# One level of Strassen's product for the FFN up projection, with the norm factor put into the activations

## The chip, the cores and the metric

The kernel runs on one core of a Trainium2 chip. The metric is device time in microseconds (us) of one execution; lower is better. Engines are named as in the profile: PE (TensorE, matmuls; PEld its weight loads), DVE (VectorE), ACT (ScalarE), POOL (GpSimd), SP (SyncE, which issues the DMAs here).

## The reference

The kernel computes a two-layer trunk over 1024 positions of width 1024 in float32. Each layer has an attention mixer and a gated FFN with a causal depthwise convolution; both layers have the same FFN, with their own weights:

```python
D_MODEL = 1024; SEQ = 1024; D_FF = 2816; CONV_WIDTH = 3

def conv_ffn(h, w_up, conv_w, conv_b, w_down):
    u = h @ w_up
    y = conv_b
    for j in range(CONV_WIDTH):
        y = y + conv_w[j] * _shift(u, CONV_WIDTH - 1 - j)
    a, g = jnp.split(y, 2, axis=-1)
    return (jax.nn.silu(g) * a) @ w_down

def reference(x, ...):
    h = x
    for i in range(DEPTH):
        n = rmsnorm(h, attn_norm_g[i])
        m = dsa_mixer(...) if i % N_MIXERS == 0 else chunk_band_mixer(...)
        h = h + m @ w_out[i]
        h = h + conv_ffn(rmsnorm(h, ffn_norm_g[i]), w_up[i], conv_w[i], conv_b[i], w_down[i])
    return h
```

## The kernel before

The program is a row of phases: `head_phase`, `select_phase`, `dsa_phase`, `ffn_phase` for layer 0, `band_phase`, `ffn_phase` for layer 1. The change concerns the two FFN phases. The residual stays in SBUF as XT, transposed: 8 blocks (db) of 128 model columns by 1024 positions.

**Arithmetic.** PE multiplies in fp32r. Each float32 operand is split into a high part (a copy by ACT to fp32r) and a low part (operand less high, by POOL or DVE), and each product is three matmuls: high x high, high weight x low activation, low weight x high activation. One matmul is 128x128 weights by 128x512 activations.

**Up projection.** The 5632 columns of w_up are 44 chunks of 128, ordered so that chunks 2m and 2m + 1 are the value and the gate of the same 128 hidden columns; two of them are called a pair here, and there are 22 pairs. `up` (L359) takes one chunk: for 8 db, 3 products and 2 halves of the positions, 48 matmuls at L375 into one of two PSUM pairs (UP), 128x1024. DVE multiplies the result by RB, the norm's factor of every position spread over the partitions, into U (L423). ACT starts Y as u times the last tap plus the bias (L283), DVE adds the two shifted taps (L425, L431), ACT applies silu to the gate (L287), DVE multiplies (L437), ACT and POOL split the product into AH and AL (L291, L330).

**Down projection.** Two pairs are a group. `down` (L381) multiplies the group's two hidden chunks: 8 db x 2 chunks x 3 x 2, 96 matmuls at L391, and DVE adds each 128x1024 result to XT (L413).

**Weights.** A ring of four chunks: SP loads WR (512 KB each, L241), ACT makes WH (L268), POOL WL (L322), two chunks ahead of PE. The order on each engine is the order in which the program writes it; engines meet by semaphores. A loop of five turns holds two groups each: 4 chunks, down of the group before, 4 chunks, down.

**Start of a phase.** XH and XL are XT times the norm's gain, split by ACT (L139) and DVE (L145). The norm's factor isn't in them: while PE multiplies, the sums of squares are joined (L160, L163), summed over partitions by sixteen small matmuls (L152), turned into a factor by DVE and POOL (L167, L172), put on diagonals (DG, L450), spread by PE (L354) and copied to RB (L277). It is needed only at L423.

Of the kernel before, what the change touches and what calls it, by code (L numbers as in the profile page):

```python
# [17 lines left out]
P = 128  # L18
D = 1024
# [12 lines left out]
UPC = 2 * PAIRS  # L32
CHUNKS = NGRP * (UPC + PAIRS)
RING = 4
# [58 lines left out]
class Squares:  # L93
# [5 lines left out]
    def __init__(self, c, sem, xsq=None):  # L99
        self.c = c  # L100
        self.XSQ = c.XSQ if xsq is None else xsq
        self.squared, self.even, self.odd = sem("squared_x"), sem("even_added"), sem("odd_added")
# [5 lines left out]
    def add(self, eng, db):  # L108
# [5 lines left out]
        acc = c.ACC[:, db % 2, :]  # L114
# [7 lines left out]
class Norm:  # L122


    def __init__(self, c, stage, m, sem, bank, last_square):
        self.c, self.stage, self.LAST = c, stage, last_square
        self.squared = sem("n_squared")
        self.VAR = m.take(f"VAR{stage}", [P, TT], F32)
# [19 lines left out]
    def tensor(self, pe):  # L148
        c = self.c
        pe.wait_ge(self.joined, 2)  # L150
        for t in range(TT):
            mm = pe.matmul(self.SS[:, t:t + 1], c.ACC[:, 0, t * P:(t + 1) * P], c.ONES[:, 0:1], start=True, stop=True)  # L152
        mm.then_inc(self.summed, 1)
# [4 lines left out]
    def join(self, dve):  # L158
        c = self.c
        dve.tensor_tensor(c.ACC[:, 0, :], c.ACC[:, 0, :], c.ACC[:, 1, :], ALU.add).then_inc(self.joined, 1)  # L160
        dve.wait_ge(self.joined, 1)
        dve.wait_ge(self.squared, 1)
        dve.tensor_tensor(c.ACC[:, 0, :], c.ACC[:, 0, :], self.LAST, ALU.add).then_inc(self.joined, 1)  # L163
# [11 lines left out]
def ffn_phase(nc, c, layer, stage, stream, out=None, w_next=None):  # L175
# [4 lines left out]
    with ExitStack() as ctx:  # L180
        sem, old = c.signals.open(ctx, f"f{layer}")
        m = Map(nc, c.scratch, c.end)
        WR = c.chunks[layer].W
        m.at += RING * 4 * D
        WH = m.take(f"WH{layer}", [P, RING, D], F32R)
        WL = m.take(f"WL{layer}", [P, RING, D], F32R)
        Y = m.take(f"Y{layer}", [P, PAIRS, 2, S], F32)
        AH = m.take(f"AH{layer}", [P, 2, PAIRS, S], F32R)
        AL = m.take(f"AL{layer}", [P, 2, PAIRS, S], F32R)
        U = m.take(f"U{layer}", [P, 2, S], F32)  # L190
        RB = m.take(f"RB{layer}", [P, S], F32)
        DG = m.take(f"DG{layer}", [P, TT, P], F32)
        norm = Norm(c, stage, m, sem, c.bank[7], Y[:, 0, 0, :])
        squares = Squares(c, sem) if out is None else None
        UP = [c.pair[1], c.pair[0]]
        DN = c.pair[2:4]
        landed = [sem(f"landed{i}") for i in range(RING)]
        w_hi, w_lo = sem("w_hi"), sem("w_lo")
        up_ready, biased, tap1, convolved = sem("up_ready"), sem("biased"), sem("tap1"), sem("convolved")
        scaled, diag_ready, spread, rb_ready = sem("scaled"), sem("diag_ready"), sem("spread"), sem("rb_ready")  # L200
# [3 lines left out]

        PER = UPC + PAIRS
        LOOPS = (NGRP - 1) // 2
        TURN = 2 * PER
        AHEAD = 2
        EARLY = c.chunks[layer].count
        assert CHUNKS == UPC + LOOPS * TURN + PAIRS and TURN % RING == 0  # L210

        def at(it, per_turn, n):

            return n if it is None else it * per_turn + n

        def up_at(n):

            return n + max(n // UPC - 1, 0) * PAIRS

        def down_at(g):  # L220

            return UPC + (g + 1) * PER - PAIRS if g < NGRP - 1 else CHUNKS - PAIRS

        def wait_weights_used(eng, it, ch):

            g, k = divmod(ch - UPC, PER)
            if ch < UPC:
                eng.wait_ge(up_ready, at(it, 2 * UPC, ch + 1))
                if it is not None:
                    eng.wait_ge(dn_free, at(it, 2 * DB, 2))  # L230
            elif k < UPC:
# [2168 lines left out]
```

## Time and profile before

| | before |
|---|---|
| median of 3 runs | 2798.01 us (2797.06 to 2799.74) |
| the profiled execution: time | 2800.03 us |
| the profiled execution: span | 2797.9 us |
| PE busy | 2700.6 us, 97% |
| DVE busy | 1426.0 us, 51% |
| ACT busy | 1118.5 us, 40% |
| POOL busy | 918.5 us, 33% |
| mean granted clock of PE | 0.989 of full speed |
| matmuls at L375 and L391 | 4224 and 2112 |

The span is the time from the first to the last instruction of the profiled execution. PE's busy time is of pipelined matmuls: one lasts 0.39 us, though the next starts earlier. The first FFN phase lies at about 694 to 1436 us, the second from 2055 us to the end.

### The profile page before, as it was taken

How to read it: one execution, taken by the hardware profiler on the slowest of the kernel's cores; microseconds unless marked ns; L12 is line 12 of the kernel's file. 1: busy time of each engine (PE TensorE's matmuls, PEld its weight loads, DVE VectorE, ACT ScalarE, POOL GpSimd, SP SyncE). 2: the span in 40 equal slices, each digit the busy share in tenths (PEclk: the TensorE clock that was granted, in tenths of full speed). 3: DMA queues.
4: the chain of work that ended last, by engine and by line, in shares of the span. 5: the costliest groups of instructions: out<-in, count | busy, mean ns of one | idle time of the engine just before them, and what ended most of it. 6: DMA issues, size and time to landing. Idle time of an engine off the chain costs nothing. (4 is left out here: it accounts for less than half of the span.)

```text
span 2797.9 us, 38917 instructions
## 1 busy us (share of the span) xinstructions
PE 2700.6 (97%) x14518; PEld 2347.8 (84%) x14518; DVE 1426.0 (51%) x2492; ACT 1118.5 (40%) x2415; POOL 918.5 (33%) x639
## 2 busy tenths in 40 slices
PE   7799899999999999999999999999989999999999
PEld 6599788887788888888889999999868888888887
DVE  5899777741554444444441114666145444444444
ACT  5687666642322222222245446777123222222221
POOL 2134433103332223322244444564223332322322
PEclk9899999999999999999999999999999999999999
DMA  5100000101111111111121111334111111111111
GB/s 175 46 29 22 24 9 9 65 27 49 46 53 53 45 45 45 53 52 45 46 101 46 46 46 30 87 90 133 38 53 46 46 47 58 45 52 45 45 52 60
DMA packets 71012, 147.13 MB, mean 53 GB/s; under 512 B 7824, under 2 KB 44864, under 8 KB 69216
## 3 DMA queue, kind: packets, MB, share of 16 engines
q1 hardware_dynamic: 70880, 145.38, 16.4%
q8 instruction: 82, 1.34, 0.2%
q14 instruction: 50, 0.41, 0.1%
HBM read 122.22 MB, written 13.69 MB: 49 GB/s over the span
## 5 line engine op out<-in xcount | busy, mean ns | idle before, releaser
L375 PE MATMUL banks<-XH,WH 128*128 128x512 f32 x1408 | 438.4, 393 | 21.3 <-POOL WL L322 12.6
L322 POOL TENSOR_TENSOR WL<-WR,WH 128x1024 fp32r<-128x1024 f32 x132 | 328.1, 2493 | 376.8 <-ACT WH L268 376.8
L375 PE MATMUL banks<-XH,WL 128*128 128x512 f32 x1408 | 436.9, 392 | 0.0
L375 PE MATMUL banks<-XL,WH 128*128 128x512 f32 x1408 | 436.5, 391 | 0.0
L283 ACT ACTIVATE Y<-U,CONVB,CONVW 128x1024 f32<-128x1024 f32 x88 | 109.5, 1244 | 630.4 <-DVE U L423 630.4
L375 PEld LDWEIGHTS banks<-XH,WH 128*128 128x128 f32 x1408 | 265.6, 189 | 79.3 <-POOL WL L322 13.4
L423 DVE TENSOR_TENSOR U<-banks,RB 128x1024 f32<-128x1024 f32 x88 | 107.7, 1224 | 410.6 <-PE banks L375 395.6
L375 PEld LDWEIGHTS banks<-XH,WL 128*128 128x128 f32 x1408 | 266.3, 189 | 55.7
L375 PEld LDWEIGHTS banks<-XL,WH 128*128 128x128 f32 x1408 | 266.1, 189 | 55.7
L330 POOL TENSOR_TENSOR AL<-Y,AH 128x1024 fp32r<-128x1024 f32 x44 | 105.9, 2407 | 608.6 <-ACT AH L291 608.6
L413 DVE TENSOR_TENSOR XT<-XT,banks 128x1024 f32<-128x1024 f32 x176 | 214.4, 1218 | 165.0 <-PE banks L391 165.0
L391 PE MATMUL banks<-AH,WH 128*128 128x512 f32 x704 | 219.3, 393 | 0.0
L391 PE MATMUL banks<-AL,WH 128*128 128x512 f32 x704 | 217.2, 390 | 0.0
L391 PE MATMUL banks<-AH,WL 128*128 128x512 f32 x704 | 216.9, 389 | 0.0
L268 ACT ACTIVATE WH<-WR 128x1024 fp32r<-128x1024 f32 x132 | 136.1, 1046 | 193.4 <-PE banks L391 101.9
L431 DVE SCALAR_TENSOR_TENSOR Y<-U,CONVW,Y 128x1022 f32<-128x1022 f32 x88 | 197.1, 2240 | 8.8 <-DVE Y L425 0.9
L425 DVE SCALAR_TENSOR_TENSOR Y<-U,CONVW,Y 128x1023 f32<-128x1023 f32 x88 | 113.0, 1284 | 137.2 <-ACT Y L283 137.2
L391 PEld LDWEIGHTS banks<-AH,WH 128*128 128x128 f32 x704 | 130.6, 188 | 31.5 <-DVE XT L413 5.5
L391 PEld LDWEIGHTS banks<-AL,WH 128*128 128x128 f32 x704 | 132.2, 188 | 27.9
L391 PEld LDWEIGHTS banks<-AH,WL 128*128 128x128 f32 x704 | 132.2, 188 | 27.8
L2092 PE MATMUL banks<-QW,XH 128*128 128x384 f32 x512 | 132.0, 338 | 16.4 <-POOL QW L2040 16.4
L1015 DVE TENSOR_SCALAR QVAR<-SSQ 128x4 f32<-128x4 f32 x64 | 20.5, 320 | 208.7 <-ACT JUNK L712 208.7
(264 smaller groups left out, 5528.5 us busy)
## 6 DMA issues: line engine op xcount, KB each, us to landing
WR<-in_ffn SPq DMA_DIRECT2D x132, 512.0 KB, 3.5
HT<-HC SPq DMA_DIRECT2D x224, 64.0 KB, 2.0
QWR<-in_qkv SPq DMA_DIRECT2D x8, 1536.0 KB, 6.5
XT<-in_xT SPq DMA_DIRECT2D x16, 512.0 KB, 7.8
OWR<-in_w_o SPq DMA_DIRECT2D x16, 512.0 KB, 3.3
QWR1F<-in_qkv SPq DMA_DIRECT2D x4, 1536.0 KB, 6.2
spill<-XT SPq DMA_DIRECT2D x8, 512.0 KB, 11.3
XT<-spill SPq DMA_DIRECT2D x8, 512.0 KB, 7.1
```

The costliest lines, as they stand in the source:

```text
L268: act.activation(WH[:, ch % RING, :], WR[:, ch % RING, :], ACT.Copy).then_inc(w_hi, 1)
L283: act.activation(Y[:, j, k, :], U[:, k, :], ACT.Identity, bias=c.CONVB[:, layer, bass.ds(tap, 1)], scale=c.CONVW[:, layer, 2, bass.ds(tap, ...
L322: pool.tensor_tensor(WL[:, ch % RING, :], WR[:, ch % RING, :], WH[:, ch % RING, :].bitcast(F32), ALU.subtract).then_inc(w_lo, 1)
L330: pool.tensor_tensor(AL[:, g % 2, j, :], Y[:, j, 0, :], AH[:, g % 2, j, :].bitcast(F32), ALU.subtract).then_inc(a_lo, 1)
L375: mm = pe.matmul(u[:, h * HALF:(h + 1) * HALF], w[:, ch % RING, db * P:(db + 1) * P], x[:, db, h * HALF:(h + 1) * HALF], start=(db == 0 an ...
L391: mm = pe.matmul(DN[db % 2][:, h * HALF:(h + 1) * HALF], w[:, (ch + j) % RING, db * P:(db + 1) * P], x[:, g % 2, j, h * HALF:(h + 1) * HAL ...
L413: dve.tensor_tensor(c.XT[:, db, :], c.XT[:, db, :], DN[db % 2][:], ALU.add).then_inc(dn_free, 1)
L423: dve.tensor_tensor(U[:, k, :], UP[k][:], RB[:], ALU.mult).then_inc(scaled, 1)
L425: dve.scalar_tensor_tensor(Y[:, j, k, 1:S], U[:, k, 0:S - 1], c.CONVW[:, layer, 1, bass.ds(tap, 1)], Y[:, j, k, 1:S], ALU.mult, ALU.add).t ...
L431: dve.scalar_tensor_tensor(Y[:, j, k, 2:S], U[:, k, 0:S - 2], c.CONVW[:, layer, 0, bass.ds(tap, 1)], Y[:, j, k, 2:S], ALU.mult, ALU.add).t ...
L1015: dve.tensor_scalar(VAR[:, t % 2, :], SSQ[:, t % 2, :], 1.0 / HD, EPS, ALU.mult, ALU.add).then_inc(var_ready, 1)
L2092: mm = pe.matmul(PJ[t % len(PJ)][:, 0:PROJ], x[:, db, i * P:(i + 1) * P], w[:, k % 2, db, :], start=(db == 0 and x is c.XH and w is WH), s ...
```

## The change

The FFN phase is written anew around `Pair`, the two chunks of one pair.

- **Seven products.** A pair's weights are 1024 model rows by 256 columns. They are cut into quarters A11, A12 (first chunk, model rows 0 to 511 and 512 to 1023) and A21, A22 (second chunk). The activations are cut into quarters too: model rows by positions 0 to 511 and 512 to 1023. One quarter product is 4 blocks x 3 = 12 matmuls into one PSUM bank. Eight would be needed; `seven` does seven, with four sums of weight quarters (POOL, L579, once per pair: 128x512 each) and four sums of activation quarters T1 to T4 (once per layer). The sums of the results are made partly by PE, which accumulates two products in one bank, and partly by DVE (`u2`, `c22`, `c21`, `c12`: 5 additions of a bank and a 128x512 piece of U) and ACT (two copies, `first_copy`, `second_copy`). Pair 0 is done with eight products (`classic`), 96 matmuls, pairs 1 to 21 with 84.
- **Norm factor.** The factor RB is now multiplied into the activations, with the gain, before they are split (`scale_x`, L771, DVE). So no activation exists before the factor does; the multiplication of the results (L423 before) is gone.
- **Weights.** Highs and lows are made for each of the seven quarters (or sums), 128x512, in a ring of six slots (WH, WL). The raw chunks are loaded into one place (RAW, two chunks), as soon as the last low of the pair before is made. Down projection weights come as four halves of 256 KB, which take four slots.
- **Order.** The loop has nine turns: seven products of a first pair, a down projection, seven products of a second pair. The next turn's first pair follows directly. After the loop come two pairs and two down projections.
- The squares' accumulators of the FFN's norm lie elsewhere (FFN_ACC); the input arrays `up` and `down` are apart. The loads of the first two chunks in the phase ahead are as before.

The core of the diff:

```diff
+UP = 7
+CLASSIC = 4
+DOWN = 4
+TURN = 2 * UP + DOWN
+SLOTS = 6
+LOOPS = NGRP - 2
+LAST = 2 * NGRP - 1
...
-        WH = m.take(f"WH{layer}", [P, RING, D], F32R)
-        WL = m.take(f"WL{layer}", [P, RING, D], F32R)
+        WH = m.take(f"WH{layer}", [P, SLOTS, HALF], F32R)
+        WF = nc.alloc_sbuf_tensor_at(f"WF{layer}", [P, SLOTS, HALF], F32, offset=m.at)
+        WL = m.take(f"WL{layer}", [P, SLOTS, HALF], F32R)
...
+        A11, A12, A21, A22 = raw(0, 0), raw(0, 1), raw(1, 0), raw(1, 1)
+        S3_AT, S4_AT = A21, A11
+        def source(pair, k):
+            return (A11, full(pair.slot + 1), full(pair.slot + 2), S3_AT, A12, A22, S4_AT)[k]
...
+            def load_pair(it, p):
+                pair, before = Pair(it, p), Pair(it, p - 1)
+                sp.wait_ge(w_lo, CLASSIC if p == 1 else before.slots(UP))
+                for k in range(2):
+                    sp.dma_start(RAW[:, k, :], up[pair.tap(k)]).then_inc(raw_landed, 16)
...
+            def upper(it, p):
+                pair, nxt, ahead = Pair(it, p - 1), Pair(it, p), Pair(it, p + 1)
+                weights_high(nxt, 4, 5)
+                bias(pair)
+                first_copy(nxt)
+                weights_high(nxt, 6)
+                silu(pair)
+                split(pair)
+                weights_high(ahead, 0)
+                second_copy(nxt)
+                weights_high(ahead, 1, 2, 3, 4)
...
+            def first_sums(pair):
+                pool.wait_ge(raw_landed, pair.at(32, 32 * pair.p))
+                wait_slot(pool, pair.it, pair.slot + 1)
+                sum_of(pair, full(pair.slot + 1), A21, A22, ALU.add)
+                pool.wait_ge(w_sum, pair.sums(1))
+                sum_of(pair, S3_AT, A11, A21, ALU.subtract)
+            def second_sums(pair):
+                wait_slot(pool, pair.it, pair.slot + 2)
+                pool.wait_ge(w_sum, pair.sums(2))
+                sum_of(pair, full(pair.slot + 2), A22, S3_AT, ALU.subtract)
+                pool.wait_ge(w_sum, pair.sums(3))
+                pool.wait_ge(w_lo, pair.slots(1))
+                sum_of(pair, S4_AT, A12, full(pair.slot + 2), ALU.subtract)
...
+            def product(pair, k, bank, i, first):
+                n = (pair.slot + k) % SLOTS
+                pe.wait_ge(w_lo, pair.slots(k + 1))
+                for b in range(4):
+                    for w, x in ((WH, XH[i]), (WL, XH[i]), (WH, XL[i])):
+                        mm = pe.matmul(BANK[bank], w[:, n, b * P:(b + 1) * P], x[:, b, :],
+                                       start=(first and b == 0 and w is WH and x is XH[i]),
+                                       stop=(b == 3 and x is XL[i]), skip_group_check=not first)
+                mm.then_inc(product_done, 1)
+            def seven(pair):
+                pe.wait_ge(copied, pair.copies(0))
+                product(pair, 0, 0, B11, True)
+                pe.wait_ge(mixed, pair.mixes(0))
+                product(pair, 1, 2, T1, True)
+                product(pair, 2, 1, T2, True)
+                product(pair, 3, 3, T3, True)
+                pe.wait_ge(copied, pair.copies(1))
+                product(pair, 4, 0, B21, False)
+                pe.wait_ge(mixed, pair.mixes(2))
+                product(pair, 5, 3, T4, False)
+                pe.wait_ge(mixed, pair.mixes(3))
+                product(pair, 6, 2, B22, False)
...
+            with pe.Fori(0, LOOPS) as it:
+                seven(Pair(it, 2))
+                lower(it, 0)
+                seven(Pair(it, 3))
...
+            def scale_x(q, b):
+                x, db, rb = x_quarter(q, b)
+                dve.scalar_tensor_tensor(scaled_x[q][:, b, :], x, c.GAIN[:, stage, db:db + 1], rb, ALU.mult,
+                                         ALU.mult).then_inc(x_scaled, 1)
+            def while_product(pair, nxt):
+                taps(pair)
+                u2(nxt)
+                gate(pair)
+                c22(nxt)
+                c21(nxt)
```

(In `seven` the waits of pair 1 for its T quarters are left out.) Three places show how the order of the work moved. The first is POOL at the loop's second half, where the second pair's last three weights are followed by the next turn's first pair. Before, a group's turn on POOL was differences (L322) and a split (L330), all 128x1024:

```order
L322 TENSOR_TENSOR WL_8864<-WR_73,WH_8863 128x1024
L322 TENSOR_TENSOR WL_8864<-WR_73,WH_8863 128x1024
L330 TENSOR_TENSOR AL_8867<-Y_8865,AH_8866 128x1024
L322 TENSOR_TENSOR WL_8864<-WR_73,WH_8863 128x1024
L322 TENSOR_TENSOR WL_8864<-WR_73,WH_8863 128x1024
L330 TENSOR_TENSOR AL_8867<-Y_8865,AH_8866 128x1024
```

Now, from the next pair's first weight on (L579 are the sums of weight quarters, WF a sum's full value, AL the split of the pair before):

```order
L563 TENSOR_TENSOR WL_8872<-WR_74,WH_8870 128x512
L579 TENSOR_TENSOR WF_8871<-WR_74 128x512
L579 TENSOR_TENSOR WR_74<-WR_74 128x512
L563 TENSOR_TENSOR AL_8893<-Y_8891,AH_8899 128x1024
L563 TENSOR_TENSOR WL_8872<-WF_8871,WH_8870 128x512
L579 TENSOR_TENSOR WF_8871<-WR_74 128x512
L579 TENSOR_TENSOR WR_74<-WR_74,WF_8871 128x512
L563 TENSOR_TENSOR WL_8872<-WF_8871,WH_8870 128x512
L563 TENSOR_TENSOR WL_8872<-WR_74,WH_8870 128x512
L563 TENSOR_TENSOR WL_8872<-WR_74,WH_8870 128x512
```

The split of the activations stands between the sums, and the third weight's difference follows the third and fourth sum. The second place is ACT at the loop's end and start: the highs of the next pair's later weights, one of which reads WF and so waits for POOL's third sum, stand ahead of the bias (L458) of the pair that PE has just finished:

```order
L464 ACTIVATE YG_8897<-YG_8897 128x1024
L469 ACTIVATE AH_8899<-Y_8891 128x1024
L414 ACTIVATE WH_8870<-WR_74 128x512
L443 ACTIVATE U_8894<-banks 128x512
L414 ACTIVATE WH_8870<-WF_8871 128x512
L414 ACTIVATE WH_8870<-WF_8871 128x512
L414 ACTIVATE WH_8870<-WR_74 128x512
L414 ACTIVATE WH_8870<-WR_74 128x512
L414 ACTIVATE WH_8870<-WR_74 128x512
L458 ACTIVATE Y_8891<-U_8894,CONVB,CONVW 128x1024
```

The third is DVE after the last quarter of the activations is scaled at a phase's start (L783 make T1, T2 and T4, L788 their lows, XQF and XQL the quarters' full and low parts):

```order
L783 TENSOR_TENSOR XQF_8887<-XQF_8889,B11F_8895 128x512 x4
L783 TENSOR_TENSOR XQF_8888<-B22F_8892,XQF_8887 128x512 x4
L788 TENSOR_TENSOR XQL_8883<-XQF_8887,XQH_8876 128x512 x4
L783 TENSOR_TENSOR XQF_8890<-B21F_8898,XQF_8888 128x512 x4
L788 TENSOR_TENSOR XQL_8884<-XQF_8888,XQH_8877 128x512 x4
L788 TENSOR_TENSOR XQL_8886<-XQF_8890,XQH_8879 128x512 x4
L821 SCALAR_TENSOR_TENSOR Y_8891<-U_8894,CONVW,Y_8891 128x1023
```

All of them stand ahead of the first pair's convolution (L821), where before the convolution followed the first result at once.

## Rows read from the trace of the kernel before

**Rows 1.** The page: busy us (share) xinstructions of PE to ACT, and the last chain.

```profile
PE 2700.6 (97%) x14518; PEld 2347.8 (84%) x14518; DVE 1426.0 (51%) x2492; ACT 1118.5 (40%) x2415; POOL 918.5 (33%) x639
...
PE 26%; DVE 0%; ACT 0%; POOL 0%; issue 0%
```

**Rows 2.** Stretches: length, busy us of PE, PEld, DVE, ACT, POOL, PEclk, DMA.

```profile
693.00:725.00 32.00, 21.44 (x78) 16.32 (x79) 20.15 (x13) 12.73 (x13) 10.53 (x4) 0.79 0.25 83
...
800.00:1425.00 625.00, 625.00 (x2751) 515.48 (x2751) 297.40 (x215) 147.60 (x137) 192.92 (x78) 1.00 0.15 46
...
2086.00:2760.00 674.00, 674.00 (x2968) 555.99 (x2967) 323.79 (x229) 162.79 (x152) 201.01 (x83) 1.00 0.15 46
```

**Rows 3.** Timeline of DVE, steady part: start, us, instruction, [idle before <- releaser].

```profile
1032.88 3.18 DVE L431 SCALAR_TENSOR_TENSOR Y<-U,CONVW,Y 128x1022 f32<-128x1022 f32 x1 [0.15 <-DVE Y L425]
1039.44 1.23 DVE L423 TENSOR_TENSOR U<-banks,RB 128x1024 f32<-128x1024 f32 x1 [3.39 <-PE banks L375]
...
1043.65 1.28 DVE L431 SCALAR_TENSOR_TENSOR Y<-U,CONVW,Y 128x1022 f32<-128x1022 f32 x1
...
1050.32 1.23 DVE L423 TENSOR_TENSOR U<-banks,RB 128x1024 f32<-128x1024 f32 x1 [3.04 <-PE banks L375]
```

**Rows 4.** Timeline of POOL at the same place.

```profile
1032.32 2.66 POOL L322 TENSOR_TENSOR WL<-WR,WH 128x1024 fp32r<-128x1024 f32 x1 [9.85 <-ACT WH L268]
```

**Rows 5.** Timeline of PE, projection of the second mixer: matmuls of 384 columns.

```profile
1481.85 0.33 PE L861 MATMUL banks<-QWH,XL 128*128 128x384 f32 x1
...
1482.89 0.34 PE L861 MATMUL banks<-QWH,XL 128*128 128x384 f32 x1
```

**Rows 6.** Groups by line and shape: xcount | busy us, mean ns | idle before.

```profile
L322 POOL TENSOR_TENSOR WL<-WR,WH 128x1024 fp32r<-128x1024 f32 x132 | 328.1, 2493 | 376.8 <-ACT WH L268 376.8
L413 DVE TENSOR_TENSOR XT<-XT,banks 128x1024 f32<-128x1024 f32 x176 | 214.4, 1218 | 165.0 <-PE banks L391 165.0
L268 ACT ACTIVATE WH<-WR 128x1024 fp32r<-128x1024 f32 x132 | 136.1, 1046 | 193.4 <-PE banks L391 101.9 <-DVE XT L413 91.5
L283 ACT ACTIVATE Y<-U,CONVB,CONVW 128x1024 f32<-128x1024 f32 x88 | 109.5, 1244 | 630.4 <-DVE U L423 630.4
L287 ACT ACTIVATE Y<-Y 128x1024 f32<-128x1024 f32 x44 | 46.7, 1061 | 141.6 <-DVE Y L431 141.6
L828 POOL TENSOR_TENSOR KL<-HT,KH 128x256 fp32r<-128x256 f32 x56 | 41.0, 732 | 4.5
L1021 DVE TENSOR_TENSOR TILE<-TILE,RS 128x256 f32<-128x256 f32 x64 | 26.6, 416 | 0.0
L697 ACT ACTIVATE QWH<-QWR 128x1536 fp32r<-128x1536 f32 x8 | 11.9, 1497 | 0.0
```

**Rows 7.** DMA issues: engine, operation xcount, KB each, median us to landing.

```profile
WR<-in_ffn SPq DMA_DIRECT2D x132, 512.0 KB, 3.5
...
QWR<-in_qkv SPq DMA_DIRECT2D x8, 1536.0 KB, 6.5
```

**Rows 8.** PE after a gap at the first FFN phase's start: timeline, and a stretch.

```profile
718.11 0.74 PE L375 MATMUL banks<-XH,WH 128*128 128x512 f32 x2 [2.04 <-DVE XL L145]
...
719.00:722.40 3.40, 3.40 (x10) 2.63 (x9) 0.00 (x0) 0.00 (x0) 0.00 (x0) 0.50 0.01 2
```

**Rows 9.** Timeline of the first FFN phase's start, from ACT's first instruction.

```profile
694.35 1.15 ACT L139 ACTIVATE XH<-XT,GAIN 128x1024 fp32r<-128x1024 f32 x1 [10.08 <-PEq L1118]
...
710.55 0.17 DVE L167 TENSOR_SCALAR VAR<-banks 128x8 f32<-128x8 f32 x1 [2.35 <-PE banks L152]
...
710.79 2.62 POOL L172 TENSOR_TENSOR RSTD<-VAR,NHALF 128x8 f32<-128x8 f32 x1 [7.27 <-DVE VAR L167]
...
724.48 1.03 ACT L277 ACTIVATE RB<-banks 128x1024 f32<-128x1024 f32 x1 [17.92 <-PE banks L354]
...
734.05 1.23 DVE L423 TENSOR_TENSOR U<-banks,RB 128x1024 f32<-128x1024 f32 x1 [1.36 <-PE banks L375]
...
755.81 1.22 DVE L423 TENSOR_TENSOR U<-banks,RB 128x1024 f32<-128x1024 f32 x1 [3.73 <-PE banks L375]
```

More of the change, by code:

```diff
@@ L193, in ffn_phase @@
-        norm = Norm(c, stage, m, sem, c.bank[7], Y[:, 0, 0, :])
-        squares = Squares(c, sem) if out is None else None
-        UP = [c.pair[1], c.pair[0]]
-        DN = c.pair[2:4]
[L197 to L200, printed above, removed]
+        RAW = c.chunks[layer].W
@@ new lines, in ffn_phase @@
+        norm = Norm(c, stage, VAR, sem, c.bank[7], Y0[:, 0, :], c.ACC)
+        squares = Squares(c, sem, acc) if out is None else None
+        BANK = c.bank[0:4]
+        DN = c.pair[2:4]
+        RB = c.pair[2]
+        uses = slot_uses()
+        raw_landed, d_landed = sem("raw_landed"), [sem(f"d_landed{d}") for d in range(DOWN)]
+        w_sum, w_hi, w_lo = sem("w_sum"), sem("w_hi"), sem("w_lo")
+        diag_ready, spread = sem("diag_ready"), sem("spread")
+        x_scaled, x_hi, x_lo_pool, x_lo_dve = sem("x_scaled"), sem("x_hi"), sem("x_lo_pool"), sem("x_lo_dve")
@@ L293, in _, with classic_high @@
[L293 to L306 removed]
+            def classic_high(n):
+                act.wait_ge(c.chunks[layer].landed, 16 * 2)
+                act.activation(high(n), CLASSIC_W[n], ACT.Copy).then_inc(w_hi, 1)
@@ new lines, in silu, with split @@
+            def silu(pair):
+                act.wait_ge(convolved, pair.at(2, 2 * pair.p + 2))
+                act.activation(Y1[:], Y1[:], ACT.Silu).then_inc(silu_done, 1)
+            def split(pair):
+                y0, ah, _ = activations(pair.p)
+                act.wait_ge(gated, pair.done())
+                act.activation(ah, y0, ACT.Copy).then_inc(a_hi, 1)
+            for n in range(CLASSIC):
+                classic_high(n)
+            norm.square_last(act)
+            first, second = Pair(None, 0), Pair(None, 1)
@@ new lines, in classic_low, with weights_low, down_low @@
+            def classic_low(n):
+                subtract(low(n), n + 1, CLASSIC_W[n], high(n), w_lo, w_hi)
+            def weights_low(pair, *which):
+                for k in which:
+                    n = pair.slot + k
+                    subtract(low(n), pair.slots(k + 1), source(pair, k), high(n), w_lo, w_hi)
+            def down_low(it, g, *which):
+                for d in which:
+                    n = down_slot(g) + d
+                    subtract(low(n), turn(it, TURN, n + 1), full(n), high(n), w_lo, w_hi)
@@ L457, in _ @@
+            for db in range(4, DB):
+                add(None, NGRP - 2, db)
             for db in range(DB):
```

690 lines of the change are left out of this document (476 added, 214 removed).

## The prediction

> **What bounds the kernel now.** I read the page's busy times first. PE is busy for 2700.6 of 2797.9 us, and the chain that ended last, which reaches back over the last FFN phase, is PE's alone, 26% of the span on L375 and L391 and nothing above 0% elsewhere [rows 1]. So time goes where PE's matmuls go. The stretches say where PE is not full: in the steady part of both FFN phases PE is busy for all of 625 and all of 674 us at clock 1.00, and each phase opens with 32 us in which it is busy for 21.4 [rows 2]. Next the pace. The 128x1024 results of the up projection leave PE every 10.88 us (1039.44 to 1050.32) for 48 matmuls, 0.2267 us each [rows 3]. The other engines wait for PE there; what they do costs nothing as long as it stays behind PE.
>
> **What is removed.** The up projection of 21 of a layer's 22 chunk pairs falls from 96 to 84 matmuls. That is 252 fewer a layer, 252 x 0.2267 = 57.1 us, 114 us for both. Will the pace hold? Now twelve matmuls in a row write one bank and each has new weights. A stage with just that pattern runs at 384 columns: six starts in 1.04 us, 0.173 each [rows 5], 0.160 for the columns at 2.4 GHz and 13 ns besides. With 512 columns that is 0.213 + 0.013, the same 0.2267. I keep it; bounds 0.22 and 0.24 move the saving by 2 us a layer.
>
> By the Trainium skill (TensorE: Matmul & The Clock Gate, section Back-to-back issue gap) a stream of weight loads and 512-column matmuls sustains about 131 ns each; by that the saving would be 504 x 0.131 = 66 us, and the sum further down 48 us higher. This trace disagrees in every stage, so the rule gets no chance.
>
> **What is added, and its durations.** Per pair POOL gets seven differences and four sums of 128x512. POOL takes 0.73 us at 256 columns and 2.49 at 1024 (2.39 undisturbed) [rows 6], so 1.28 between them. ACT's copies take 1.046 at 1024 and 1.497 at 1536, so 0.59 at 512; bias 1.24, silu and a full-width split 1.06 [rows 6]. DVE gets five combining additions a pair, of one PSUM bank and one SBUF tile: 0.416 at 256 and 1.218 at 1024 give 0.69. The four convolution steps stay at 1.28, the gate product at 1.23.
>
> The row that matters most is a wait in DVE. L431 takes 1.28 us at 1043.65 and 3.18 at 1032.88 [rows 3]; in the second case POOL ran L322 from 1032.32 to 1034.98 [rows 4], and DVE ended 1.08 us after it. POOL in turn took 2.66 there and not 2.4, since DVE was still in L425. An operation of DVE with two SBUF inputs and one of POOL exclude each other for the whole instruction. L413, with one input in PSUM, has a mean of 1218 over 176 and is never held up [rows 6]. So combining additions and residual additions are free of it; the convolution steps, the gate and the activation differences are not. With POOL's queue full, every such step of DVE costs 1.28 + 1.08 - 0.14 = 2.2 us (0.14 is POOL's early start).
>
> **A turn, followed.** A turn of the loop is pair A (19.04 us), the down projection (21.76), pair B (19.04): 59.8 us of matmuls for 65.3 before. Weights have six slots. The down projection gives everybody time, so B starts with four of its seven weights ready. The critical place is B followed by the next A. Clock it from B's first matmul:
> - ACT: two weight highs, then bias at 2.5. DVE's four steps on A's results, with two of POOL's differences in between, end at 9.6; silu 10.7, gate 12.0, split 13.1, and only then, by ACT's order, the high of the next A's first weight, 13.7. Raw weights are there: asked for at 7.1 when B's last low is done, and one 512 KB load takes 3.5 us, 1536 KB 6.5 [rows 7], so two take 5.0.
> - POOL: first low, two sums, the 2.4 us split, second low, third sum: 5 x 1.28 + 2.4, done at 22.5. The fourth sum and the third low follow, 25.0; PE wants it at 19.04 + 2 x 2.72 = 24.5. A stall of 0.5.
> - ACT: the high of the third weight had to wait for that third sum; it and three more come before bias of B by ACT's order, so 22.5 + 4 x 0.57 = 24.7, bias 25.9.
> - DVE: POOL now has five differences queued, and each step pays for one: 27.3, 29.6, 31.8, 34.0; silu 35.1, gate 36.4, first combination of bank 3 at 37.1.
> - PE: the sixth product accumulates on that bank and wants to start at 33.2. **A stall of 4.0 us.**
>
> PE then has its clock lowered. After a gap of 2.04 us that ended at 718.11 the granted clock was 0.50, that is 1.2 GHz, from 719.0 to 722.4 [rows 8]; 3.4 us at half speed lose 1.7 us. So the place costs 0.5 + 4.0 + 1.7 = 6.2 us, where 5.4 are saved in a turn: a turn goes from 65.3 to 66.0. Lower bound 1.5 (one lock wait instead of four), upper bound 10 (DVE pays two of POOL's queued operations for each step).
>
> **Phase start.** Before, the first 96 matmuls are done 39.7 us after ACT's first instruction (694.35 to 734.05) and 192 at 61.5 (755.81) [rows 9]. Now nothing can be scaled before the norm factor: 3.3 us for ACT's five instructions, 5.1 with a blocked join, 2.4 for the sixteen small matmuls (DVE's idle 2.35 before VAR), 2.6 at most for the power, DG 1.2, the spread 2.2 (722.28 to 724.48): 14 us [rows 9]. Then sixteen scalings at 0.7 and eight differences with lock waits at 1.4 take DVE to 35; PE's classic pair of 96 matmuls, running behind them, ends at 39.5. So up to there nothing is lost, because PE stood still before as well. After it DVE has 24 additions and differences of 0.69 for T1, T2 and T4, and POOL twelve of 1.28, all excluding each other: T1's low is ready at about 50 (PE wants it at 42), T2's at 60.5, T4's at 63.5. Product three ends at 63.2, and DVE's convolution steps for the first pair start only then, so the sixth product waits until 74; with two low clocks the second pair ends at 82. That is 20.5 us later than before, 23.2 against the full saving. Bounds: 8 if nothing excludes anything, 33 with every operation blocked.
>
> **Others.** The second pair's junction with the third is like the ones above, 5 us (1 to 7). The last two pairs: bias of the last but one waits for all weight lows, to free its buffer, combination at 15.7 for 13.6, 3 us with the clock (1 to 6). The next phase's head weights are loaded about 7 us later in layer 0, hidden under the last down projection's 21.8 us: if not, up to 7. The multiplication by RB (L423) and its wait go, from DVE, off the path: 0.
>
> **Sum per layer:** -57.1 + 23.2 + 9 x 6.2 + 5 + 3 = +29.9; twice that is +60. The profiled execution took 2800.0 us with a span of 2797.9, the median is 2 us lower: 2798 + 60 = **2858 us**.
>
> **Rivals.**
> - *The chain closes in time* (faster). If the nine junctions cost 2.5 us each, stalls under 2 us and a clock that stays at 2.4 GHz, and the start 18 us: -57.1 + 18 + 22.5 + 4 = -12.6 a layer, 2773; with 1.5 at each, a start of 8 and 1 for each of the others, 2731. It turns at (57.1 - 23.2 - 8) / 9 = 2.9 us a junction. For it: every duration is short, and PE's lead is six products, 16 us. Against: POOL and ACT are served strictly in order and the chain above has no slack left.
> - *The shared port bounds* (slower still). POOL's 16.5 us and DVE's 6.4 for a pair are 22.9, more than PE's 19.04; over a turn, with four differences more, it is 50.9 of 59.8, so it only holds where pairs touch. If POOL keeps the port through its queued operations, a junction costs 10: +68 more, 2926. The Trainium skill (SBUF — State Buffer, section SBUF: two separate sides) calls it an exclusive lock for the whole instruction, which the rows bear out; what happens with a queue waiting on both sides no row shows.
> - *Starts only*: junctions as computed, the clock not lowered, start 12: -57.1 + 12 + 40.5 + 6 = +1.4 a layer, 2801, no change.
>
> **Chances.** Forecast 0.50 (2815 to 2900), faster rival 0.32, port 0.13, no change 0.05. About 0.2% (5.6 us) is what a measurement of this kernel can tell. Faster 0.33, same 0.05, slower 0.62. The range takes in the forecast's own and reaches down to 2762, half way between the two cases of the first rival, and up to 2905; about 1 in 10 is left out at either end.
>
> **What would show it.** Right: PE idle before the product into bank 3 of every pair A, ended by DVE's combination (L803 or L805), about 18 times at 3 to 5 us; granted clock below 1.00 inside both FFN phases; PE idle for T1 and T2; the steps of DVE (L821) with a mean near 1.9 us; matmuls still 0.2267 apart. Wrong: PE without gaps between the start and the end of the phases (first rival), or waits on POOL's weight lows everywhere (second).

## The result and the profile after

The changed kernel takes 2890.0 us (median of 4 runs, 2887.6 to 2892.5) where the kernel before takes 2797.5: a ratio of 1.033, 95% interval 1.031 to 1.035, slower. The forecast was 2858 us, slower, in a range of 2762 to 2905. The profiled execution took 2887.6 us, its span is 2885.8 against 2797.9 before. Of all executions below one was slow (3711.4 us at a granted clock of 0.653, of the last experiment's kernel); it is left out wherever times are compared.

The page of the changed kernel: busy times, the granted clock in 40 slices, the last chain, and the groups that answer to [rows 1, 6].

```profile
PE 2653.7 (92%) x14014; PEld 2289.1 (79%) x14014; DVE 1536.7 (53%) x2694; ACT 1263.9 (44%) x2811; POOL 1449.5 (50%) x1097
...
PEclk9899999998899999999999999999989999999999
...
issue 9%; PE 8%; POOL 5%; DVE 4%; ACT 1%; ACTq 0%; POOLq 0%; DVEq 0%
...
L702 PE MATMUL banks<-XQH,WH 128*128 128x512 f32 x1176 | 486.5, 414 | 129.3 <-DVE U L803 86.3
...
L821 DVE SCALAR_TENSOR_TENSOR Y<-U,CONVW,Y 128x1023 f32<-128x1023 f32 x80 | 150.8, 1885 | 154.8 <-ACT Y L458 149.4
...
L579 POOL TENSOR_TENSOR WF<-WR 128x512 f32<-128x512 f32 x84 | 112.2, 1335 | 140.6 <-PE banks L748 126.8
```

PE has 504 matmuls fewer, which are 114 us at 0.2267 each, and only 47 us less busy time: its mean granted clock is 0.961 where it was 0.989, so part of it runs slower. The last chain, PE's alone before [rows 1], now passes through every engine. The largest wait of PE is for DVE's combination of bank 3 (L803): 22 times, 86.3 us in all. The convolution steps (L821) have a mean of 1885 ns where one takes 1.28 alone [rows 3].

The stretches of the changed kernel (columns as in [rows 2]): the start, the steady part of both layers, then the same 9.4 us behind two stalls.

```profile
693.00:780.00 87.00, 60.98 (x219) 46.10 (x219) 66.42 (x63) 35.82 (x58) 60.10 (x39) 0.78 0.08 25
780.00:1429.00 649.00, 599.52 (x2527) 487.29 (x2526) 321.34 (x271) 207.03 (x298) 414.88 (x275) 0.96 0.15 47
...
2121.00:2770.00 649.00, 594.64 (x2496) 481.89 (x2496) 349.74 (x298) 214.38 (x314) 419.95 (x278) 0.95 0.14 44
```

```profile
860.58:870.00 9.42, 9.42 (x31) 7.56 (x32) 1.98 (x3) 2.51 (x5) 7.71 (x6) 0.72 0.18 63
927.63:937.05 9.42, 9.42 (x35) 7.74 (x36) 1.98 (x3) 3.14 (x6) 8.64 (x7) 0.84 0.17 58
```

PE was busy for the whole of the steady part before [rows 2]; now it stands for 50 to 54 us of 649, at 0.96 and 0.95 of its clock. Now one junction, pair B to the next pair A, in the changed kernel. First GpSimd (POOL), then ScalarE (ACT), VectorE (DVE) and TensorE (PE).

```profile
907.99 2.39 POOL L563 TENSOR_TENSOR AL<-Y,AH 128x1024 fp32r<-128x1024 f32 x1
...
911.60 1.28 POOL L579 TENSOR_TENSOR WF<-WR 128x512 f32<-128x512 f32 x1
...
915.45 8.01 POOL L563 TENSOR_TENSOR WL<-WR,WH 128x512 fp32r<-128x512 f32 x4
```

```profile
913.00 0.63 ACT L414 ACTIVATE WH<-WF 128x512 fp32r<-128x512 f32 x1 [5.60 <-POOL WF L579]
...
915.10 1.23 ACT L458 ACTIVATE Y<-U,CONVB,CONVW 128x1024 f32<-128x1024 f32 x1
```

```profile
909.58 0.69 DVE L813 TENSOR_TENSOR U<-banks,U 128x512 f32<-128x512 f32 x1 [2.03 <-PE banks L702]
916.48 1.37 DVE L821 SCALAR_TENSOR_TENSOR Y<-U,CONVW,Y 128x1023 f32<-128x1023 f32 x1 [6.21 <-ACT Y L458]
918.00 2.09 DVE L821 SCALAR_TENSOR_TENSOR Y<-U,CONVW,Y 128x1022 f32<-128x1022 f32 x1 [0.15 <-DVE Y L821]
920.01 4.53 DVE L821 SCALAR_TENSOR_TENSOR YG<-U,CONVW,YG 128x1023 f32<-128x1023 f32 x2
...
925.67 1.23 DVE L832 TENSOR_TENSOR Y<-Y,YG 128x1024 f32<-128x1024 f32 x1 [0.52 <-ACT YG L464]
926.81 0.68 DVE L803 TENSOR_TENSOR U<-banks,U 128x512 f32<-128x512 f32 x1
```

```profile
915.56 0.50 PE L702 MATMUL banks<-XQH,WH 128*128 128x512 f32 x1 [0.58 <-POOL WL L563]
...
923.63 0.39 PE L702 MATMUL banks<-XQL,WH 128*128 128x512 f32 x1
927.63 0.79 PE L702 MATMUL banks<-XQH,WH 128*128 128x512 f32 x1 [3.61 <-DVE U L803]
```

Pair A's first product begins at 909.4, 84 matmuls of 0.2267 us behind the start of pair B at 890.34; B's last combination (L813) is released then, too. Read down from there. The third sum ends 3.5 us into pair A (911.60 + 1.28). ACT's high of it ends the 5.6 us in which ACT stood, three more follow, then the bias at 915.10. POOL has its lows queued from 915.45, and the second to fourth step of DVE take 2.1 to 2.3 us each. The steps end 15.2 us into pair A and the gate 17.5. L803 begins at 926.81; PE had been ready for its result since 923.86 (the last matmul's start and 0.23), and starts at 927.63, 3.8 us later.

### The profile page after: what moved, and what is told of

Its sections match the earlier page's. It is cut to its first block and busy times, and to the rows that moved or that the text cites. A ratio compares the mean times of both kernels' runs of the same rounds, so it can differ in the third digit from the quotient of the medians.

```text
span 2885.8 us, 40600 instructions
## 1 busy us (share of the span) xinstructions
PE 2653.7 (92%) x14014; PEld 2289.1 (79%) x14014; DVE 1536.7 (53%) x2694; ACT 1263.9 (44%) x2811; POOL 1449.5 (50%) x1097
## 5 line engine op out<-in xcount | busy, mean ns | idle before, releaser
L702 PE MATMUL banks<-XQH,WH 128*128 128x512 f32 x1176 | 486.5, 414 | 129.3 <-DVE U L803 86.3
L563 POOL TENSOR_TENSOR WL<-WR,WH 128x512 fp32r<-128x512 f32 x218 | 342.7, 1590 | 341.1 <-ACT WH L414 324.4
L702 PE MATMUL banks<-XQH,WL 128*128 128x512 f32 x1176 | 477.0, 406 | 0.0
L702 PE MATMUL banks<-XQL,WH 128*128 128x512 f32 x1176 | 476.6, 405 | 0.0
L702 PEld LDWEIGHTS banks<-XQH,WH 128*128 128x128 f32 x1176 | 234.0, 199 | 199.7 <-issue 105.1
L702 PEld LDWEIGHTS banks<-XQH,WL 128*128 128x128 f32 x1176 | 234.4, 199 | 49.0
L702 PEld LDWEIGHTS banks<-XQL,WH 128*128 128x128 f32 x1176 | 232.3, 198 | 51.6
L563 POOL TENSOR_TENSOR WL<-WF,WH 128x512 fp32r<-128x512 f32 x172 | 252.6, 1474 | 35.8 <-ACT WH L420 35.8
L821 DVE SCALAR_TENSOR_TENSOR Y<-U,CONVW,Y 128x1023 f32<-128x1023 f32 x80 | 150.8, 1885 | 154.8 <-ACT Y L458 149.4
L414 ACT ACTIVATE WH<-WR 128x512 fp32r<-128x512 f32 x210 | 123.9, 619 | 223.1 <-PE banks L748 148.6
L579 POOL TENSOR_TENSOR WF<-WR 128x512 f32<-128x512 f32 x84 | 112.2, 1335 | 140.6 <-PE banks L748 126.8
L821 DVE SCALAR_TENSOR_TENSOR YG<-U,CONVW,YG 128x1023 f32<-128x1023 f32 x88 | 151.4, 1721 | 5.3
```

What stands on the lines that cost most here:

```text
L414: act.activation(high(pair.slot + k), source(pair, k), ACT.Copy).then_inc(w_hi, 1)
L563: pool.tensor_tensor(out_, src, hi.bitcast(F32), ALU.subtract).then_inc(signal, 1)
L579: pool.tensor_tensor(target, x, y, op).then_inc(w_sum, 1)
L702: mm = pe.matmul(BANK[bank], w[:, n, b * P:(b + 1) * P], x[:, b, :], start=(first and b == 0 and w is WH and x is XH[i]), stop=(b == 3 and ...
L821: dve.scalar_tensor_tensor(y[:, lag:S], u[:, 0:S - lag], c.CONVW[:, layer, 2 - lag, bass.ds(n, 1)], y[:, lag:S], ALU.mult, ALU.add).then_i ...
```

## The experiments

All are edits of the changed kernel; the ratios are to the kernel before.

### Does the stall come from the order on ScalarE?

```diff
                 second_copy(nxt)
-                weights_high(ahead, 1, 2, 3, 4)
+                weights_high(ahead, 1)
+                bias(nxt)
+                weights_high(ahead, 2, 3, 4)
...
                 weights_high(nxt, 5)
-                bias(pair)
```

> ScalarE's bias step of pair B stands one place earlier: behind the high part of the next pair's second weight, ahead of those of its third to fifth (it stood behind all of them). Theory of the prediction (the step waits for the third weight sum of GpSimd only because of ScalarE's order; with it the convolution steps and the combination are late): the bias ends about 4 us earlier, VectorE's four steps each still pay a blocked 2.2 us, the combination comes at about the time at which TensorE wants it. The stall of 3.8 us before the product into bank 3 and most of the lowered clock behind it go at the 10 junctions of a layer: 20 x 5.5 = 110 us, so about 2780 (2765 to 2810), idle time ended by L803 down from 86 us to under 20, mean clock over 0.98. Rival (GpSimd's queue of differences is what holds VectorE up, whenever its steps begin): the steps only begin earlier and last longer, at most 30 us are gained, 2858 or more, and the waits on L803 stay over 50 us.

Measured: 2839.3 us, ratio 1.014 (1.012 to 1.016). A turn takes 62.6 or 64.2 us for 66.0 or 67.1. Waits of PE and a junction of this kernel, POOL and then PE:

```profile
PE banks L702 <- POOL WL L563: 50.7, 20, 3.6
...
PE banks L702 <- DVE U L803: 15.8, 4, 5.3
```

```profile
904.95 1.30 POOL L579 TENSOR_TENSOR WF<-WR 128x512 f32<-128x512 f32 x1
906.33 2.15 POOL L579 TENSOR_TENSOR WR<-WR,WF 128x512 f32<-128x512 f32 x1
908.44 2.24 POOL L563 TENSOR_TENSOR WL<-WF,WH 128x512 fp32r<-128x512 f32 x1
```

```profile
907.94 0.39 PE L702 MATMUL banks<-XQL,WH 128*128 128x512 f32 x1
910.74 0.50 PE L702 MATMUL banks<-XQH,WH 128*128 128x512 f32 x1 [2.41 <-POOL WL L563]
```

Both theories got something right. The order did it: 18 of 22 waits on L803 are gone. But the steps now begin at 905.3, before POOL has made the fourth sum and the third low, and here POOL pays for the exclusion: 2.15 and 2.24 us where 1.30 was usual. PE waits 2.4 us for the low instead. So 51 us were gained and not 110. The wait on L803 fell by 70.5 us and the wait on POOL's lows rose by 38.5 (12.2 in the changed kernel); that accounts for 32 of the 51, and the lowered clock, 0.969 in the mean for 0.961, costs less as well.

### Is it the third weight sum?

```diff
                 first_sums(ahead)
-                split(pair)
                 weights_low(ahead, 1)
                 second_sums(ahead)
+                split(pair)
                 weights_low(ahead, 2, 3, 4)
```

> GpSimd's 2.4 us split of the gated activations (L839's twin on GpSimd, the instruction into AL) moves behind the last two weight sums; nothing else is changed. Theory of the prediction: the third sum comes 2.4 us earlier, with it the third to fifth weight highs, the bias, the steps and the combination; the stall of 3.8 us shrinks to about 1.4 and the short one on the third weight low (0.6 to 0.7) goes: 20 x 3.1 = 62 us, to 90 us if the clock is then no longer lowered: 2800 to 2826. Rival (the chain is not bound by the third sum): only the short stall goes, 20 x 0.7 = 14 us, 2874 or more.

Measured: 2830.7 us, ratio 1.011 (1.010 to 1.013), 59 us less than the change. That is near the 62 us computed for the stalls alone, though just outside the range given, and it is near by luck. The wait on L803 halved (43.1 us in place of 86.3), which the rival did not expect. But the short stall, which was to go, grew (33.4 us for 12.2, 20 times), because the split now stands ahead of the third low. Both waits together give only 22 us; the rest came with the clock, which stays up here (below) and costs 2.0 us a turn by the next experiment. A turn is 63.3 us in all of the loop. In its steady part this kernel stands and does not slow down: after a gap of 1.61 us the matmuls still start 0.23 apart, and the granted clock is 1.00 in this row of its stretches.

```profile
870.00:1335.00 465.00, 445.00 (x1946) 363.97 (x1945) 252.38 (x206) 153.20 (x218) 306.59 (x203) 1.00 0.15 49
```

### What does the lowered clock cost?

```diff
+                if pair.p == 2:
+                    filler(pair)
                 pe.wait_ge(mixed, pair.mixes(2))
```

> TensorE gets 16 matmuls of 512 columns (3.6 us at 0.2267) into a bank that nobody reads, ahead of its wait for the combination in each pair A of the loop (9 a layer). The arithmetic of the kernel is unchanged. Theory of the prediction (TensorE stands still for 3.8 us and then runs at half its clock for some 3.4 us, which loses 1.7): the filler fits into the idle time and costs nothing, the clock stays at 1.00 behind it: 18 x 1.7 = 31 us less, about 2858 (2850 to 2868), idle on L803 down by some 60 us. Rival (the low clock has another cause, or costs nothing since others are waited for): the same time as without it, 2888, or up to 15 us more where the filler is longer than the stall.

Measured: 2848.9 us, ratio 1.018 (1.017 to 1.020), 41 us less for 288 matmuls more. In its trace the 16 fillers (into c.pair[2]) take the place of the stall, and the next product goes on at full speed (the changed kernel had starts 0.43 apart here).

```profile
918.64 3.79 PE L711 MATMUL banks<-XQH,WH 128*128 128x512 f32 x16
922.34 0.50 PE L702 MATMUL banks<-XQH,WH 128*128 128x512 f32 x1
922.68 0.39 PE L702 MATMUL banks<-XQH,WL 128*128 128x512 f32 x1
```

The stall itself is about as long as before (from matmul to matmul 918.41 to 922.34, for 923.63 to 927.63), so all that was gained is the clock: 2.0 us a turn (64.56 for a mean of 66.56), and 2.7 us ahead of the first residual addition of layer 0. I had taken 1.7. The two stretches above say why: every second turn has 12 slow matmuls and not 7.

### What sets the start?

```diff
+                T = [B11] * 4 if early else [T1, T2, T3, T4]
...
                 if early:
                     pe.wait_ge(copied, 2)
-                    pe.wait_ge(t_lo_dve, 4)
...
-                product(pair, 1, 2, T1, True)
+                product(pair, 1, 2, T[0], True)
```

> Pair 1, the first one with seven products, uses the first activation quarter for its four T products as well and waits for none of the T quarters (its part of the result is left wrong); they are still made at the same places, and pair 2 waits for them. Theory of the prediction (VectorE's queue sets the start: the T differences, then four convolution steps, only then the combination): TensorE runs ahead and stops before its sixth product until the same moment, so at most 3 us a layer are gained, 2882 to 2890. Rival (the T quarters' readiness is what TensorE waits for at the start, 8.5 + 4.8 us a layer): pair 1 ends about 13 to 17 us earlier in each layer, 2855 to 2862.

Measured: 2889.3 us, ratio 1.033 (1.031 to 1.035), the time of the change. PE's waits for the T quarters are worth nothing, since VectorE comes to its combination no sooner. The second run takes the work itself away.

```diff
-            t_made(T1, TF[T3], B11F, 0)
-            t_made(T2, B22F, TF[T1], 4)
-            t_low(T1, 0)
...
-            t_low(T4, 12)
```

> The making of the T quarters of the activations is left out: 24 differences of 128x512 on VectorE, 8 on GpSimd and 16 high parts on ScalarE in each layer; all products take the first quarter in their place (results left wrong), TensorE has the same matmuls. Theory of the prediction (the start is set by these differences, on two engines that exclude each other, ahead of the first convolution steps on VectorE): the first two pairs then need no more than 40 + 19 = 59 us after ScalarE's first instruction instead of 81, about 20 us a layer, 2850 (2843 to 2858). Rival (the start is lost in the norm factor and its sixteen scalings, ahead of the first matmul): at most 5 us a layer, 2878 or more.

Measured: 2844.0 us, ratio 1.017 (1.015 to 1.018). The first residual addition comes at 783.2 and not at 804.5: 21 us in layer 0, 46 in all. The norm factor and the scalings ahead of the first matmul are hardly a part of the loss: in the changed kernel the first pair's 96 matmuls are done 41.3 us after ScalarE's first instruction (735.92 less 694.63), where it was 39.7.

### Two reorderings that gave little

```diff
                 u2(nxt)
-                gate(pair)
                 c22(nxt)
+                gate(pair)
                 c21(nxt)
```

> VectorE combines bank 3 and bank 2 of the next pair (L803, L805) ahead of the gate product of the pair before, no longer behind it; nothing else changes. Theory: the combination was only late by what stands ahead of it on VectorE; it loses the silu and the gate, 1.1 + 1.2 us, from its chain, but not the convolution steps. The stall goes from 3.8 to 1.5 us: 20 x 2.3 = 46 us, up to 70 if the clock then stays up: 2818 to 2845. It was 8.0 us at the last but one pair, where silu itself was late: that stall goes nearly whole, 2 x 6 us, contained in the range. Rival (the port: VectorE's and GpSimd's work is a fixed sum, so an order changes nothing): 2875 or more.

Measured: 2872.1 us, ratio 1.027 (1.025 to 1.029). 18 us were gained, where one theory gave 45 to 70 and the other at most 15. L803 costs 41.1 us, as expected, but a late gate makes a late split on ScalarE, behind which stands the next pair's first weight high, and from there on the chain comes later. POOL's lows cost PE 37.8 us for 12.2, and the down projection waits for the split.

```diff
-                weights_high(ahead, 1, 2, 3, 4)
+                weights_high(ahead, 1, 2)
+                bias(nxt)
+                weights_high(ahead, 3, 4)
...
                 weights_low(nxt, 5, 6)
+                split(Pair(it, 0))
```

The lines that take the moved steps from their old places (`bias(pair)` on ACT, `split(pair)` on POOL) are not shown, nor is the silu that is moved in the tail.

> Orders only, arithmetic as in the change: ScalarE's bias behind the next pair's third weight high (not its second as in bias_early, where that weight's low came 2.4 us late); GpSimd's split of pair A behind the following pair's sixth and seventh weight low; at the end of the phase ScalarE's silu of the last but two pair ahead of the last pair's first weight high, which waits for a load. Theory: the third sum is done 2.4 us earlier, its weight high and low follow before the convolution steps begin, the bias comes 3 to 4 us earlier; both stalls of a junction fall under 1 us and the clock stays at 1.00. Of 6.7 us a junction 5.5 or more are gained, 20 x 5.5 = 110, and 8 us in each tail: 2770 (2755 to 2790), under the 2798 of the kernel before. Rival (VectorE's steps and GpSimd's queue block each other wherever they stand, and what one gains the other loses, as bias_early's 50.7 us on the weight lows): no better than the 2831 of split_late, at least 2815.

> As combo2, and VectorE's combinations ahead of the gate as in gate_late. Theory: a stall of 0.5 to 1 us is left in combo2 before the product into bank 3; the gate's place takes it away: 5 to 20 us under combo2. Rival: nothing is left there, the two agree within 3 us.

Measured: 2854.8 us, ratio 1.020 (1.018 to 1.022), and with the gate moved 2849.6, 1.018 (1.017 to 1.020). Computed were 2770: by these two alone the rival, a fixed sum of blocking work, looked right. Moving the gate gave 5 us, the least of what was expected. The trace of the first (combo2) shows what my sum had left out, POOL and then DVE:

```profile
899.13 1.30 POOL L562 TENSOR_TENSOR WL<-WR,WH 128x512 fp32r<-128x512 f32 x1 [7.74 <-ACT WH L414]
...
917.11 2.37 POOL L562 TENSOR_TENSOR AL<-Y,AH 128x1024 fp32r<-128x1024 f32 x1
```

```profile
917.12 3.43 DVE L832 TENSOR_TENSOR Y<-Y,YG 128x1024 f32<-128x1024 f32 x1 [0.53 <-ACT YG L464]
```

The moved split hit the gate, which took 3.43 us for 1.23. And POOL had stood idle for 7.7 us ahead of a low that waited for a high, with the sums queued behind it that needed only the raw weights. So the work does not fill the time.

### The sums first

```diff
                 weights_low(nxt, 4, 5, 6)
-                weights_low(ahead, 0)
                 first_sums(ahead)
-                split(pair)
-                weights_low(ahead, 1)
-                second_sums(ahead)
-                weights_low(ahead, 2, 3, 4)
+                third_sum(ahead)
+                weights_low(ahead, 0)
+                fourth_sum(ahead)
+                weights_low(ahead, 1, 2, 3, 4)
...
                 weights_low(nxt, 5, 6)
+                split(Pair(it, 0))
```

On ScalarE the first weight high comes before the split, and the bias behind the fifth.

> Orders only, from combo2's trace: there GpSimd stood idle for 7.7 us before the first weight low of the next pair A, while the raw weights had landed at about 896 us and the third sum was done only at 905.5; and its split of pair A (2.4 us, one instruction) fell on the gate, which took 3.43 us. Now GpSimd makes the first three weight sums before that pair's first weight low and the split of pair A behind its seventh low; ScalarE takes the high of the first weight before the split and those of the second to fifth before the bias. The bias then waits for nothing but the last combination (0.7 us into pair A) and comes at 904.6 instead of 906.2, with only three of GpSimd's lows left to block VectorE's steps. Theory of the prediction (a chain of waits, which a better order closes): the combination comes at most 2 us late: 20 x (3.8 + 1.7 - 2) = 70 and the shorter stalls 20 x 0.7 besides, tails 10: 2795 (2775 to 2815). Rival (around a junction the two engines' blocking work is more than TensorE's time, whatever the order): between 2825 and 2855 like all orders so far.

> As sums_first4g, and VectorE's combination ahead of the gate. Theory: the stall of up to 2 us before the product into bank 3 goes, and the split that the down projection waits for is still in time, since all of it began 1.5 to 3 us earlier than in combo3, where TensorE waited 2.25 us a turn for it: 15 to 50 us under sums_first4g, so 2765 (2745 to 2790), faster than the kernel before. Rival (fixed sum of work): what is gained at the combination is lost at the down projection's wait for the split, and the two differ by less than 8 us.

Measured: 2789.9 us, ratio 0.996 (0.995 to 0.998), and with the combination ahead of the gate 2766.3, 0.989 (0.987 to 0.991). The chain was a matter of order. A turn of the second takes 60.6 us, where 59.8 are matmuls; its steady stretch, and its only wait in a turn, for the split:

```profile
870.00:1335.00 465.00, 461.69 (x2030) 380.09 (x2029) 266.49 (x217) 162.37 (x232) 331.22 (x213) 1.00 0.16 52
```

```profile
914.96 0.72 PE L755 MATMUL banks<-AH,WH 128*128 128x512 f32 x2 [0.47 <-POOL AL L562]
```

POOL is busier here than in the changed kernel's same stretch (331.2 for 294.1 us), and PE waits for nothing else.

### The tail, and the start once more

```diff
             first_sums(last)
-            third_sum(last)
             weights_low(last, 0)
+            third_sum(last)
             fourth_sum(last)
-            weights_low(last, 1, 2)
-            split(pair)
-            weights_low(last, 3, 4, 5, 6)
+            weights_low(last, 1, 2, 3, 4, 5, 6)
+            split(pair)
```

> sums_first4 with another order in the tail of each layer alone. There bias of the last but one pair waits for all seven weight lows of the last one (its buffer lies on the raw weights), and GpSimd's 2.4 us split stood before four of them: bias at 1351.0 us, TensorE idle 6.05 at 1359.8. The split now follows the lows, and the third sum the first low (TensorE had waited 1.1 us for that low). Theory: 2.4 + 1.1 us a layer, 7 us in all: 2759 (2755 to 2763). Rival (the loads of the raw weights set the tail): within 3 us of sums_first4, 2764 or more.

Measured: 2760.3 us, ratio 0.986 (0.984 to 0.988), 6 us less than sums_first4, as computed (7).

```diff
             for b in range(4):
-                pool.wait_ge(t_dve, b + 1)
-                pool.tensor_tensor(TF[T3][:, b, :], B22F[:, b, :], TF[T3][:, b, :], ALU.subtract).then_inc(t_pool, 1)
...
+            for b in range(4):
+                dve.wait_ge(t_dve, b + 1)
+                dve.tensor_tensor(TF[T3][:, b, :], B22F[:, b, :], TF[T3][:, b, :], ALU.subtract).then_inc(t_pool, 1)
```

> tail_order, and GpSimd's eight differences for the third T quarter made by VectorE. In sums_first4 VectorE's 24 differences, GpSimd's eight and five instructions on weights lie between 729.8 and 761.6 us: 24 x 0.65 + 13 x 1.28 = 32.2 for a measured 31.8. Theory (the two engines exclude each other, and the start is the sum of their times): 32 x 0.65 + 5 x 1.28 = 27.2, 4 to 5 us less a layer, so 6 to 10 us under tail_order. Rival (they overlap in truth, and VectorE is merely slow): VectorE gets 5.2 us more work a layer, 5 to 10 us over tail_order.

Measured: 2756.9, 2757.3 and 2762.4 us, ratio 0.986 (0.984 to 0.988), no difference from tail_order (2759.6 to 2761.7) that can be told. Neither side of the expectation came out. The trace shows why, DVE and then POOL:

```profile
728.81 6.87 DVE L784 TENSOR_TENSOR XQF<-XQF,B11F 128x512 f32<-128x512 f32 x4
735.60 2.48 DVE L784 TENSOR_TENSOR XQF<-B22F,XQF 128x512 f32<-128x512 f32 x4
738.01 2.48 DVE L789 TENSOR_TENSOR XQL<-XQF,XQH 128x512 fp32r<-128x512 f32 x4
...
752.46 4.51 DVE L822 SCALAR_TENSOR_TENSOR Y<-U,CONVW,Y 128x1023 f32<-128x1023 f32 x2
```

```profile
739.35 14.31 POOL L562 TENSOR_TENSOR WL<-WR,WH 128x512 fp32r<-128x512 f32 x1 [4.22 <-ACT WH L414]
```

VectorE ends its differences at 752.5 and not at 761.6, with eight more of them: the exclusion, not their number, makes that stretch long. But one low of POOL, 1.28 us long alone, was shut out for 14.3 us, and PE then waited for it. The product into bank 3 begins 6.2 us earlier than in tail_order (762.83 for 768.99), the first residual addition only 1.7 (795.10 for 796.76).

## Why the prediction was right, and where its sizes were off

- **What is removed.** The pace held: starts 0.2267 apart, a product every 2.72 us.
- **The junction.** The chain was right in every link. On pair A's clock (first product at 0, 909.38): third sum 3.5 us (forecast 3.5), first bias ended 7.0 (6.9), the four steps 15.2 (15.0), gate 17.5 (17.4), the combination of bank 3 ended 18.1 (18.1). bias_early, split_late and sums_first4 each took the cause away from another side, and the stall went or shrank. That the steps pay for POOL's queue, one operation each, is in the 2.1 to 2.3 us of L821, and bias_early showed the reverse side, which the sum had not: a step of VectorE also makes POOL's sums and lows late.
- **The clock.** Right in kind; 2.0 us a junction and not 1.7 (filler). With stalls of 0.74 and 3.75 a turn takes 66.56 us for 59.84 of matmuls, so a junction costs 6.7 for a forecast of 6.2: 8 turns, 4 us a layer.
- **The second pair's junction with the third** cost 6.9 us and not 5 (L813 at 775.86 and 801.75, 25.9 us for 19.04).
- **The start.** The second pair's last combination begins at 775.86, when its last product ends: 81.2 us after ScalarE's first instruction at 694.63; forecast 82. PE stood 8.5 us before the product with T1 (until 747.29) and 4.8 before that with T2 (until 757.52). t_nowait and t_none confirm that it is the making of the T quarters on VectorE and GpSimd, and not PE's wait for them, that sets the start.
- **The end of the phase** holds the terms that were mis-sized. From the last turn's first residual addition (1336.93) to the last (1473.28) are 136.4 us for 119.7 of matmuls, 16.7 lost, where 6.2 + 3 were forecast. Most of it is the ninth of the "9 x 6.2": that junction was taken to be like the eight others, and cost 11.2 by an estimate from PE's starts (0.74 and 8.2 of stalls, the rest slow matmuls). PE stood 8.2 us there, until 1397.50, and not 3.75. ScalarE's silu of the pair before stands behind a weight high of the last pair, whose load had only been asked for at 1388.92, when the last low of the pair ahead was done; so silu came 4.4 us after the steps' end (1389.9). In combo2, where silu stands ahead of that high, the stall at this place is 3.2 us, as at its other junctions (3.3). But the tail as a whole took 136.1 us there, since the last pair's waits grew; what would shorten it is not shown by that run. The last pair's own term, "bias of the last but one waits for all weight lows", was right in kind (ScalarE's bias at 1411.79 had waited 2.25 us for POOL's low): PE stood 3.1 us and ran slow behind it, 5.2 us for 3 by the same count.

```profile
1393.79 0.63 ACT L414 ACTIVATE WH<-WR 128x512 fp32r<-128x512 f32 x1 [9.89 <-DMA WR<-in_up]
1394.33 1.04 ACT L464 ACTIVATE YG<-YG 128x1024 f32<-128x1024 f32 x1
```

```profile
1397.50 0.79 PE L702 MATMUL banks<-XQH,WH 128*128 128x512 f32 x1 [8.03 <-DVE U L803]
```

- **The sum.** Layer 0, from ScalarE's first instruction to the last addition: 778.7 us for 737.7, +41.0 (forecast +29.9). The terms above give 4.1 + 1.9 + 7.5 - 0.8 = 12.7 us of a difference of 11.1; 1.6 stay unassigned. Layer 1 +41.3. The phases between give 5.4 more, 2.1 of it in longer waits of PE for ScalarE there (5.4 for 3.3 us); the cause of the rest is open. So the forecast was 60 us slower and 92 were measured, inside the range, with the direction and the mechanism right and every junction a little dearer than computed. The range itself has a slip: its lower end, 2762, is called half way between the rival's 2773 and 2731, which is 2752.
- **The rivals.** *The chain closes in time* was wrong for this kernel, though one order of the same instructions makes it true. *The shared port bounds*: no; in the changed kernel a step waits for one of POOL's queued operations, not for all of them, and sums_first4 does the same work in 60.6 us a turn. *Starts only*: no, the clock was lowered and the start cost its full forecast. The Trainium skill (SBUF — State Buffer, section SBUF: two separate sides) says that whoever starts first keeps the port for a whole instruction and the other blocks; the 2.1 us steps and the 2.24 us low agree. The rule does not say whom it lets in when both have a queue (last section).

## What to carry to other kernels

Saved matmuls pay only if the helpers' chain closes: follow one junction by hand, on one clock, engine by engine in its own order, and ask of each instruction that waits what stands behind it. When moving one step brings half of the forecast, look where an engine stands idle ahead of work that is ready, before calling the work too much: here orders alone were worth 130 us (2890 to 2760) and turned a loss of 3.3% into a gain of 1.4%. In a chain in which two engines exclude each other, do the slow one's work before the other's burst begins, and look at the end of a loop by itself: an instruction that waits for a load there holds up what stands behind it.

## What was not expected of the hardware

- An instruction of POOL can be shut out for as long as VectorE goes on without a gap: 14.31 us for 1.28 in t3_on_vector, under 22 differences of VectorE that started 0.60 us apart. When POOL had its queue full ahead of VectorE, the two took turns, and the same instructions took 1.72 us each (728.81, 6.87 us for four). Who was there first does not settle it: in the changed kernel a low of POOL came at 744.97 upon VectorE's differences, which had started 0.60 us apart since 743.63, and was let in at once (1.67 us; VectorE's next difference took 1.75). No run separates the cases.
- Stalls that look alike leave different traces in the clock. Behind 3.6 us of idle time 7 matmuls were slow in one turn and 12 in the next. In bias_early, behind 2.4 us, seven starts of matmuls followed each other 0.43 apart at one junction, from the sixth matmul on (910.74), and at the next none did (974.92). Behind 1.61 and 1.2 to 1.3 us (split_late) none was.
